# A hybrid decoder block: the gated activations transposed by VectorE in 32x32 squares and by transfers inside SBUF

## The chip, the cores and the metric

The kernel runs on one core of a Trainium2 chip. The metric is device time in microseconds. The core has TensorE (PE, matmul), VectorE (DVE), ScalarE (ACT), GpSimd (POOL) and SyncE (SP, here only an issuer of DMAs); each runs its own instruction stream, and they wait for each other by semaphores.

## The reference

One decoder block over 256 tokens of width 2048, in float32: a gated feed-forward (FFN), a mixer with a convolution group and an attention group, a second FFN, and a final norm. The change is in the two FFNs:

```python
D_MODEL = 2048
SEQ = 256
D_FF = 5632
...
def swiglu(h, wg, wu, wd):
    return (jax.nn.silu(h @ wg) * (h @ wu)) @ wd
...
        x = x + 0.5 * swiglu(rmsnorm(x, ffn1_norm[i]), ffn1_wg[i], ffn1_wu[i], ffn1_wd[i])
        x = x + hybrid_mixer(rmsnorm(x, mix_norm[i]), w_in[i], ...)
        x = x + 0.5 * swiglu(rmsnorm(x, ffn2_norm[i]), ffn2_wg[i], ffn2_wu[i], ffn2_wd[i])
    return rmsnorm(x, final_norm)
```

## The kernel before

**Products in three parts.** Every large product is made of float32r matmuls, with both operands split into a high and a low part: hi x hi, hi x lo and lo x hi (L459, L460, L461). The activations stand transposed in SBUF as the stationary operand (hT_hi, hT_lo for the input of a layer; guT_hi, guT_lo for silu(gate) times up), and the weights stream by as the moving operand.

**Weights in groups.** A group is 256 rows of a weight matrix by 512 columns, 512 KB. Four slots hold groups in three buffers: raw, w_hi, w_lo. SyncE loads a group into raw as soon as VectorE has made w_lo of the group four before it (`load`, L348). ScalarE copies raw to w_hi (`hi`, L841) when the load has landed and TensorE is done with the group four before. VectorE subtracts to get w_lo (`lo`, L1164). TensorE then runs the group's 12 matmuls (`group`, L459 to L461): two row blocks, two token tiles, three products.

**An FFN.** The hidden width is 11 chunks of 512 columns (NFC = 11). For a chunk there is a "gate" job and an "up" job of 8 groups each (JD = 8); gate goes to PSUM banks 0 and 1, up to banks 2 and 3. A hardware loop of 10 passes (`Fori`) holds the up job of chunk i and then the gate job of chunk i + 1; the up job of the last chunk and the "down" jobs (22 groups each, JF = 22, four column blocks) follow behind it. Each engine has the same order of groups written out by hand, with its own side work put in behind a numbered group: `after={1: [...]}` runs something behind group 1 of the job.

**A chunk's side work.** When the gate job is done, ScalarE makes silu of it into gu (`silu`, L887, [128 tokens, 2 tiles, 512]), behind group 1 of the up job. When the up job is done, VectorE multiplies gu by it (`up`, L1213), behind group 1 of the next gate job. Behind group 3 of that gate job TensorE transposes gu with eight 128x128 transposes into banks 4 and 5 (`gu_transposes`, L480 through `transposes`). Behind group 5, ScalarE copies the banks to guT_hi (`gu_operand`, L895) and VectorE subtracts to guT_lo (L1221). For the last chunk the same steps stand in the first down job. The down jobs read guT_hi and guT_lo, and the last chunk's tiles only from group 18 of the first down job on.

```python
                with pe.Fori(0, NFC - 1) as i:
                    job(c, JD, hT_hi, hT_lo, 1, i, 2 * JD)

                    pe.wait_ge(silu_done, count(2 * (NFC * f + 1), i, 2))
                    job(c + JD, JD, hT_hi, hT_lo, 0, i, 2 * JD, after={3: [lambda: gu_transposes(f, 0, i)]})
```

**SyncE's queue** holds nothing but loads in the FFNs: 16 in a loop pass, in the order in which TensorE uses them, each behind its wait for w_lo.

Of the kernel before, what the change touches and what calls it, by code (L numbers as in the profile page):

```python
# [12 lines left out]
P = 128  # L13
TOK = 256
# [15 lines left out]
NCP = 16  # L30
EPS = 1e-6
# [13 lines left out]
Q0, Q1, KS, KW, KC, CC_UP, CH_UP, CB_UP, CH_LO, CB_LO, CC_LO = range(N_IN)  # L45

# [50 lines left out]
def mixer_banks():  # L97
# [20 lines left out]
    first = {4: NDC + NFC + NDC, 5: NDC + NFC + NDC, 6: 0, 7: 0}  # L118
# [12 lines left out]
def build_program(nc, a, out):  # L131
    USE, EXTRA, seen = mixer_banks()

    X_USE = {4: (0, NDC + NFC, seen[4]), 5: (0, NDC + NFC, seen[5])}
    GU_USE = {4: (NDC, seen[4] + NDC), 5: (NDC, seen[5] + NDC)}

    def operand_use(kind, which, b, n=0):

        return {"x": X_USE, "gu": GU_USE}[kind][4 + b][which] + n

# [54 lines left out]
    gu = sb("gu", [P, NT, CH])  # L195

# [64 lines left out]
    with ctx:  # L261
# [28 lines left out]
        gu_done = sem("gu_done")  # L290
        resid_done = sem("resid_done")
# [50 lines left out]
        def _(sp):  # L342
# [17 lines left out]

            def ffn(f):
# [6 lines left out]
                with sp.Fori(0, NFC - 1) as i:  # L368
                    for j in range(JD):
                        load(c + j, wu[f][:, GK * j:GK * j + GK, bass.ds(i * CH, CH)], i, 2 * JD)  # L370
                    for j in range(JD):
                        load(c + JD + j, wg[f][:, GK * j:GK * j + GK, bass.ds(i * CH + CH, CH)], i, 2 * JD)
                c += 2 * JD * (NFC - 1)
# [3 lines left out]
                for n in range(NDC):  # L377
# [3 lines left out]
                    for j in range(JF):  # L381
                        load(c + JF * n + j, wd[f][:, GK * j:GK * j + GK, n * CH:n * CH + CH])

# [60 lines left out]
        def _(pe):  # L444
# [38 lines left out]
            def x_transposes(which, n):  # L483
# [5 lines left out]
                for b in range(2):  # L489
# [4 lines left out]
                    to_bank(4 + b, operand_use("x", which, b, n))  # L494
# [3 lines left out]
            def x_operand(which, j):  # L498

                pe.wait_ge(free[4 + j % 2], operand_use("x", which, j % 2, j // 2) + 1)  # L500

            def gu_transposes(f, n, i=None):
                pe.wait_ge(gu_done, count(2 * (NFC * f + n + 1), i, 2))
                for b in range(2):
                    to_bank(4 + b, operand_use("gu", f, b, n), i, 1)
                    transposes(4 + b, [(kk * TOK + t * P, gu[:, t, (2 * b + kk) * P:][:, 0:P])
                                       for kk in range(2) for t in range(NT)])

            def gu_operand(f, j):
                pe.wait_ge(free[4 + j % 2], operand_use("gu", f, j % 2, j // 2) + 1)  # L510
# [12 lines left out]
            def ffn(f):  # L523
# [11 lines left out]
                with pe.Fori(0, NFC - 1) as i:  # L535
# [3 lines left out]
                    job(c + JD, JD, hT_hi, hT_lo, 0, i, 2 * JD, after={3: [lambda: gu_transposes(f, 0, i)]})  # L539
# [4 lines left out]
                for n in range(NDC):  # L544
                    if n == 0:
                        before = {0: [lambda: gu_operand(f, JF - 4), lambda: gu_operand(f, JF - 3)]}
                        before.update({j: [lambda j=j: gu_operand(f, j)] for j in (JF - 2, JF - 1)})
                        after = {3: [lambda: gu_transposes(f, NFC - 1)]}
                        if f == 0:
                            after[6] = [vector_transposes]  # L550
                    else:
                        before = {}
                        if f == 0:
# [265 lines left out]
        def _(act):  # L819
# [39 lines left out]
            def x_operand(which, n, b=None):  # L859
                vec0 = (V_FFN1, V_MIX, V_FFN2)[which]  # L860
                for b in range(2) if b is None else (b,):
                    scaled_operand(hT_hi, 4 * n + 2 * b, vec0, [(4 + b, operand_use("x", which, b, n))])
# [17 lines left out]
            def silu(f, n, c, i=None):  # L880
# [3 lines left out]
                for b in range(2):  # L884
                    act.wait_ge(full[4 + b], count(operand_use("gu", f, b, n), i, 1))
# [4 lines left out]
            def gu_operand(f, n, i=None):  # L890
                for b in range(2):
                    act.wait_ge(full[4 + b], count(operand_use("gu", f, b, n) + 1, i, 1))
                    k = 4 * n + 2 * b
                    dst = guT_hi[:, k:k + 2, :] if i is None else guT_hi[:, bass.ds(i * 4 + k, 2), :]
                    act.activation(dst, ps[:, 4 + b, :].rearrange("p (k t) -> p k t", k=2),  # L895
                                   ACT.Copy).then_inc(operand_hi, 1)

            def ffn(f):
# [19 lines left out]
                with act.Fori(0, NFC - 1) as i:  # L918
                    job(c, JD, i, 2 * JD, after={1: [lambda: silu(f, 0, c, i)]})
                    job(c + JD, JD, i, 2 * JD, after={5: [lambda: gu_operand(f, 0, i)]})  # L920
# [3 lines left out]
                for n in range(NDC):  # L924
                    if n == 0:
                        after = {5: [lambda: gu_operand(f, NFC - 1)]}
                        if f == 0:
                            after[8] = [vectors]
# [219 lines left out]
        def _(dve):  # L1148
# [25 lines left out]
            OP_X = {0: 0, 1: 2 * (NDC + NFC), 2: 2 * (NDC + NFC + NDC + 2)}  # L1174
            OP_GU = [2 * NDC, OP_X[2] + 2 * NDC]
            OP_ATT = 2 * (NDC + NFC + NDC)
# [39 lines left out]
            def gu_operand(f, n, i=None):  # L1216
                for b in range(2):
                    dve.wait_ge(operand_hi, count(OP_GU[f] + 2 * n + b + 1, i, 2))
                    k = 4 * n + 2 * b
                    sl = slice(k, k + 2) if i is None else bass.ds(i * 4 + k, 2)  # L1220
                    tt(guT_lo[:, sl, :], ps[:, 4 + b, :].rearrange("p (k t) -> p k t", k=2),  # L1221
                       guT_hi[:, sl, :].bitcast(F32), ALU.subtract).then_inc(free[4 + b], 1)
# [19 lines left out]
            def ffn(f):  # L1242
# [13 lines left out]
                with dve.Fori(0, NFC - 1) as i:  # L1256
                    job(c, JD, i, 2 * JD)
                    job(c + JD, JD, i, 2 * JD, after={1: [lambda: up(f, 0, c + JD, i)],
                                                      5: [lambda: gu_operand(f, 0, i)]})
# [3 lines left out]
                for n in range(NDC):  # L1263
                    if n == 0:
                        after = {1: [lambda: up(f, NFC - 1, c)], 5: [lambda: gu_operand(f, NFC - 1)]}
# [424 lines left out]
```

## Time and profile before

| | |
|---|---|
| timed runs | 1924.78 us median of 3 (1923.17 to 1926.34) |
| span of the profiled execution | 1920.8 us |
| PE, PEld busy | 1906.4 us (99%), 1562.8 us (81%) |
| DVE, ACT busy | 997.9 us (52%), 899.3 us (47%) |
| granted TensorE clock, mean | 0.999 |
| DMA | 350.96 MB, mean 183 GB/s |
| transposes of gu on PE (L480) | 176, in 22 blocks of eight |

The profile is one execution, taken by the hardware profiler. PE is the matmuls, PEld the weight loads that overlap them. DVE is VectorE, ACT is ScalarE, SPq is the issue of a DMA by SyncE. A busy PE is not PE at its peak: matmuls overlap, so the distance from one start to the next is what one costs, not its duration. A group of rows reads: line, engine, operation, output and inputs, shapes, count, busy time and mean duration, then the idle time of the engine just before them and who ended it.

### The profile page before, as it was taken

How to read it: one execution, taken by the hardware profiler on the slowest of the kernel's cores; microseconds unless marked ns; L12 is line 12 of the kernel's file. 1: busy time of each engine (PE TensorE's matmuls, PEld its weight loads, DVE VectorE, ACT ScalarE, POOL GpSimd, SP SyncE). 2: the span in 40 equal slices, each digit the busy share in tenths (PEclk: the TensorE clock that was granted, in tenths of full speed). 3: DMA queues.
4: the chain of work that ended last, by engine and by line, in shares of the span. 5: the costliest groups of instructions: out<-in, count | busy, mean ns of one | idle time of the engine just before them, and what ended most of it. 6: DMA issues, size and time to landing. Idle time of an engine off the chain costs nothing.

```text
span 1920.8 us, 23438 instructions
## 1 busy us (share of the span) xinstructions
PE 1906.4 (99%) x8715; PEld 1562.8 (81%) x8715; DVE 997.9 (52%) x1070; ACT 899.3 (47%) x1127; POOL 15.5 (1%) x24
## 2 busy tenths in 40 slices
PE   9999999999999999999999999999999999999998
PEld 7888888888888888887778778888888888888886
DVE  5445544544544444556665776544544445445444
ACT  6444444544444444444454546445444444444443
POOL 1000000000000000000000000000000000000000
PEclk9999999999999999999999999999999999999999
DMA  7555665566555556554435645665565555566664
GB/s 257 192 189 183 188 197 183 179 199 191 190 183 197 196 189 193 172 171 129 114 95 169 187 158 166 199 195 175 187 202 191 192 189 176 196 219 195 192 192 144
DMA packets 185947, 350.96 MB, mean 183 GB/s; under 512 B 13140, under 2 KB 17984, under 8 KB 185760
## 3 DMA queue, kind: packets, MB, share of 16 engines
q1 hardware_dynamic: 183264, 349.22, 56.8%
q8 instruction: 40, 0.66, 0.1%
q10 hardware_dynamic: 2240, 0.47, 0.1%
q0 software_dynamic: 384, 0.47, 0.1%
q14 instruction: 19, 0.16, 0.0%
HBM read 348.01 MB, written 2.10 MB: 182 GB/s over the span
## 4 chain that ended last, share of the span: by engine, by line
PE 97%; DVE 2%; ACT 1%; issue 0%; ACTq 0%; DVEq 0%
PE ps L459 30%; PE ps L461 30%; PE ps L460 30%; PE ps L480 3%; PE ps L625 1%; PE ps L645 1%; DVE w_lo L1164 1%; PE ps L626 0%; ACT w_hi L841 0%; PE ps L519 0%; PE ps L718 0%; DVE p_h L1433 0%; ACT junk L868 0%; DVE x L1229 0%; ACT hT_hi L855 0%
## 5 line engine op out<-in xcount | busy, mean ns | idle before, releaser
L1164 DVE TENSOR_TENSOR w_lo<-raw,w_hi 128x1024 fp32r<-128x1024 f32 x656 | 789.7, 1223 | 662.0 <-ACT w_hi L841 659.7
L841 ACT ACTIVATE w_hi<-raw 128x1024 fp32r<-128x1024 f32 x656 | 682.0, 1060 | 593.3 <-PE ps L461 517.2
L459 PE MATMUL ps<-w_hi,hT_hi 128*128 128x512 f32 x1760 | 690.9, 393 | 1.2 <-DVE w_lo L1164 1.1
L461 PE MATMUL ps<-w_hi,hT_lo 128*128 128x512 f32 x1760 | 685.6, 390 | 0.0
L460 PE MATMUL ps<-w_lo,hT_hi 128*128 128x512 f32 x1760 | 685.3, 389 | 0.0
L459 PEld LDWEIGHTS ps<-w_hi,hT_hi 128*128 128x128 f32 x1760 | 330.8, 188 | 69.1 <-issue 1.4
L461 PEld LDWEIGHTS ps<-w_hi,hT_lo 128*128 128x128 f32 x1760 | 330.4, 188 | 69.1
L460 PEld LDWEIGHTS ps<-w_lo,hT_hi 128*128 128x128 f32 x1760 | 330.7, 188 | 66.5
L459 PE MATMUL ps<-w_hi,guT_hi 128*128 128x512 f32 x704 | 274.5, 390 | 0.0
L461 PE MATMUL ps<-w_hi,guT_lo 128*128 128x512 f32 x704 | 274.0, 389 | 0.0
L460 PE MATMUL ps<-w_lo,guT_hi 128*128 128x512 f32 x704 | 273.9, 389 | 0.0
L461 PEld LDWEIGHTS ps<-w_hi,guT_lo 128*128 128x128 f32 x704 | 132.2, 188 | 27.7
L460 PEld LDWEIGHTS ps<-w_lo,guT_hi 128*128 128x128 f32 x704 | 132.2, 188 | 27.3
L459 PEld LDWEIGHTS ps<-w_hi,guT_hi 128*128 128x128 f32 x704 | 132.2, 188 | 27.1
L1221 DVE TENSOR_TENSOR guT_lo<-ps,guT_hi 128x512 f32 (+1 forms) x44 | 28.4, 686 | 96.9 <-ACT guT_hi L895 96.9
L895 ACT ACTIVATE guT_hi<-ps 128x512 f32 (+1 forms) x44 | 23.9, 594 | 108.1 <-PE ps L480 108.1
L1213 DVE SCALAR_TENSOR_TENSOR gu<-ps,rs,gu 128x512 f32<-128x512 f32 x44 | 31.0, 746 | 70.6 <-PE ps L461 70.6
L887 ACT ACT_TABLE_LOAD x20 | 25.7, 1283 | 86.7 <-PE ps L461 86.7
L1006 ACT ACTIVATE prob<-ps,mins 128x128 f32<-128x128 f32 (+1 forms) x64 | 26.3, 417 | 79.9 <-DVE mins L1378 79.9
L1183 DVE SCALAR_TENSOR_TENSOR hT_lo<-ps,vecs,hT_hi 128x256 fp32r<-128x256 f32 x48 | 20.0, 477 | 36.6 <-ACT hT_hi L855 36.6
L855 ACT ACTIVATE hT_hi<-ps,vecs 128x256 fp32r<-128x256 f32 x48 | 18.9, 475 | 39.1 <-PE ps L480 39.1
L887 ACT ACTIVATE gu<-ps,rs 128x512 f32<-128x512 f32 x44 | 27.8, 685 | 8.9 <-PE ps L461 8.6
(197 smaller groups left out, 799.7 us busy)
## 6 DMA issues: line engine op xcount, KB each, us to landing
raw<-in_ffn_wg_dram SPq DMA_DIRECT2D x176, 512.0 KB, 4.5
raw<-in_ffn_wu_dram SPq DMA_DIRECT2D x176, 512.0 KB, 4.5
raw<-in_ffn_wd_dram SPq DMA_DIRECT2D x176, 512.0 KB, 4.7
raw<-in_w_in_dram SPq DMA_DIRECT2D x88, 512.0 KB, 3.8
raw<-in_w_out_dram SPq DMA_DIRECT2D x32, 512.0 KB, 4.5
raw<-in_cmp_k_w_dram SPq DMA_DIRECT2D x8, 256.0 KB, 3.3
raw<-in_cmp_v_w_dram SPq DMA_DIRECT2D x8, 256.0 KB, 4.0
out_dram<-y_fin SPq DMA_DIRECT2D x8, 256.0 KB, 3.1
```

Of the source, the lines that this page charges most:

```text
L459: mm(o, x_hi, w_hi[:, s, kk, :], start=first and kk == 0, stop=False)
L460: mm(o, x_hi, w_lo[:, s, kk, :], start=False, stop=False)
L461: ins = mm(o, x_lo, w_hi[:, s, kk, :], start=False, stop=last and kk == GK - 1)
L480: ins = pe.transpose(ps[:, bank, o:o + P], src, ident)
L841: act.activation(w_hi[:, c % SLOTS, :, :], raw[:, c % SLOTS, :, :], ACT.Copy).then_inc(hi_ready, 1)
L887: act.activation(gu[:, t, :], ps[:, t, :], ACT.Silu, scale=rs[:, RS_FFN2 if f else RS_FFN1, t:t + 1]).then_inc(silu_done, 1)
L895: act.activation(dst, ps[:, 4 + b, :].rearrange("p (k t) -> p k t", k=2), ACT.Copy).then_inc(operand_hi, 1)
L1006: ins = act.activation(prob[:, m % 2, br * nk:br * nk + nk], ps[:, bank, br * nk:br * nk + nk], ACT.Exp, bias=mins[:, m, br:br + 1], scale ...
L1164: tt(w_lo[:, s, :, :], raw[:, s, :, :], w_hi[:, s, :, :].bitcast(F32), ALU.subtract).then_inc(lo_ready, 1)
L1183: ins = stt(out=lo_t[:, k, :], in0=ps[:, bank, kk * TOK:kk * TOK + TOK], scalar=vecs[:, vec0 + k:vec0 + k + 1], in1=hi_t[:, k, :].bitcast( ...
L1213: stt(out=gu[:, t, :], in0=ps[:, 2 + t, :], scalar=rs[:, RS_FFN2 if f else RS_FFN1, t:t + 1], in1=gu[:, t, :], op0=ALU.mult, op1=ALU.mult) ...
L1221: tt(guT_lo[:, sl, :], ps[:, 4 + b, :].rearrange("p (k t) -> p k t", k=2), guT_hi[:, sl, :].bitcast(F32), ALU.subtract).then_inc(free[4 + ...
```

## The change

gu is no longer transposed by TensorE. VectorE transposes it in squares of 32x32 (`gu_transpose`, behind group 2 of the gate job, two instructions of 128x512, from gu into gu_sq). That leaves each square transposed within its own 32 partitions. SyncE then moves the squares to the partitions where they belong, with 16 DMAs from SBUF to SBUF (`gu_blocks`): for each of the 4 x 4 pairs of partition blocks one DMA of 32 partitions, two tiles and 512 bytes, 32 KB, from gu_sq to gu_raw. They stand in SyncE's queue behind load 6 of the gate job (GU_MOVE), behind a wait for gu_squares. ScalarE copies gu_raw to guT_hi in one instruction, behind group 7 of the gate job (before: from PSUM in two, behind group 5), and VectorE subtracts to guT_lo in one. TensorE waits for gu_done at the end of the gate job, ahead of the next up job, and for gu_lo ahead of the down jobs. For the last chunk the transposes are behind group 2, the moves behind load 6 and the copies behind group 8 of the first down job. The counts of uses of banks 4 and 5 are adapted. The core of the diff (left out: the counts of bank uses, and the names of semaphores):

```diff
@@ -28,6 +28,8 @@
 CMP_BLOCK, CMP_STRIDE, CMP_HID = 32, 16, 256
 NCMP = (TOK - CMP_BLOCK) // CMP_STRIDE + 1
 NCP = 16
+SQ = 32
+QB = P // SQ
 EPS = 1e-6
 BIG = 1e30
...
@@ -43,6 +45,9 @@
 
 IN_COL = [3072, 3584, 4608, 5120, 4096, 2560, 512, 1536, 0, 1024, 2048]
 Q0, Q1, KS, KW, KC, CC_UP, CH_UP, CB_UP, CH_LO, CB_LO, CC_LO = range(N_IN)
+
+
+GU_MOVE = 6
 
 
 def mixer_order():
...
@@ -193,6 +197,8 @@
     guT_hi = sb("guT_hi", [P, KF, TOK], F32R)
     guT_lo = sb("guT_lo", [P, KF, TOK], F32R)
     gu = sb("gu", [P, NT, CH])
+    gu_sq = sb("gu_sq", [P, NT, CH])
+    gu_raw = sb("gu_raw", [P, NT, QB, CH // QB])
 
     at[0] = zone
     y_at = at[0]
...
@@ -358,6 +368,14 @@
                     sp.dma_start(x[:, :, 0:lo], x_in[:, :, 0:lo]).then_inc(x_half_landed, 16)
                 sp.dma_start(x[:, :, lo:n * CH + CH], x_in[:, :, lo:n * CH + CH]).then_inc(x_landed[n], 16)
 
+            def gu_blocks(f, n, i=None):
+
+                sp.wait_ge(gu_squares, count(NFC * f + n + 1, i, 1))
+                for a_ in range(QB):
+                    for c_ in range(QB):
+                        sp.dma_start(gu_raw[c_ * SQ:c_ * SQ + SQ, :, a_, :],
+                                     gu_sq[a_ * SQ:a_ * SQ + SQ, :, c_ * P:c_ * P + P]).then_inc(gu_moved, 16)
+
             def ffn(f):
                 c = FFN0[f]
                 for j in range(JD):
...
@@ -370,6 +388,8 @@
                         load(c + j, wu[f][:, GK * j:GK * j + GK, bass.ds(i * CH, CH)], i, 2 * JD)
                     for j in range(JD):
                         load(c + JD + j, wg[f][:, GK * j:GK * j + GK, bass.ds(i * CH + CH, CH)], i, 2 * JD)
+                        if j == GU_MOVE:
+                            gu_blocks(f, 0, i)
                 c += 2 * JD * (NFC - 1)
                 for j in range(JD):
                     load(c + j, wu[f][:, GK * j:GK * j + GK, (NFC - 1) * CH:FF])
...
@@ -380,6 +400,8 @@
                         sp.dma_start(g_fin[:, :], a["final_norm"].partition_broadcast(P)).then_inc(g_fin_landed, 16)
                     for j in range(JF):
                         load(c + JF * n + j, wd[f][:, GK * j:GK * j + GK, n * CH:n * CH + CH])
+                        if n == 0 and j == GU_MOVE:
+                            gu_blocks(f, NFC - 1)
 
             ffn(0)
             for (job, j), c in AT.items():
...
@@ -491,23 +513,13 @@
                         pe.wait_ge(gains_landed, 16)
                         pe.transpose(ps[:, 6, 0:KD], vec_rows[0:KD, :], consts[0:KD, 0:KD]).then_inc(vecs_full, 1)
                         pe.wait_ge(x_landed[0], 16)
-                    to_bank(4 + b, operand_use("x", which, b, n))
+                    to_bank(4 + b, operand_use(which, b, n))
                     transposes(4 + b, [(kk * TOK + t * P, x[:, t, (4 * n + 2 * b + kk) * P:][:, 0:P])
                                        for kk in range(2) for t in range(NT)])
 
             def x_operand(which, j):
 
-                pe.wait_ge(free[4 + j % 2], operand_use("x", which, j % 2, j // 2) + 1)
-
-            def gu_transposes(f, n, i=None):
-                pe.wait_ge(gu_done, count(2 * (NFC * f + n + 1), i, 2))
-                for b in range(2):
-                    to_bank(4 + b, operand_use("gu", f, b, n), i, 1)
-                    transposes(4 + b, [(kk * TOK + t * P, gu[:, t, (2 * b + kk) * P:][:, 0:P])
-                                       for kk in range(2) for t in range(NT)])
-
-            def gu_operand(f, j):
-                pe.wait_ge(free[4 + j % 2], operand_use("gu", f, j % 2, j // 2) + 1)
+                pe.wait_ge(free[4 + j % 2], operand_use(which, j % 2, j // 2) + 1)
 
             def vector_transposes():
...
@@ -536,20 +548,24 @@
                     job(c, JD, hT_hi, hT_lo, 1, i, 2 * JD)
 
                     pe.wait_ge(silu_done, count(2 * (NFC * f + 1), i, 2))
-                    job(c + JD, JD, hT_hi, hT_lo, 0, i, 2 * JD, after={3: [lambda: gu_transposes(f, 0, i)]})
+                    job(c + JD, JD, hT_hi, hT_lo, 0, i, 2 * JD)
+
+                    pe.wait_ge(gu_done, count(2 * (NFC * f + 1), i, 2))
                 c += 2 * JD * (NFC - 1)
                 job(c, JD, hT_hi, hT_lo, 1)
                 c += JD
                 pe.wait_ge(silu_done, 2 * NFC * (f + 1))
                 for n in range(NDC):
                     if n == 0:
-                        before = {0: [lambda: gu_operand(f, JF - 4), lambda: gu_operand(f, JF - 3)]}
-                        before.update({j: [lambda j=j: gu_operand(f, j)] for j in (JF - 2, JF - 1)})
-                        after = {3: [lambda: gu_transposes(f, NFC - 1)]}
+                        before = {0: [lambda: pe.wait_ge(gu_lo, NFC * f + NFC - 1)],
+                                  JF - 2: [lambda: pe.wait_ge(gu_lo, NFC * f + NFC)]}
+                        after = {}
                         if f == 0:
                             after[6] = [vector_transposes]
                     else:
                         before = {}
+                        if n == 1:
+                            pe.wait_ge(gu_done, 2 * NFC * (f + 1))
                         if f == 0:
                             after = {3: [lambda: x_transposes(1, n - 1)]}
                         else:
...
@@ -881,19 +897,17 @@
 
                 act.wait_ge(group_done, count(c, i, 2 * JD))
                 act.wait_ge(rs_done, (RS_FFN2 if f else RS_FFN1) + 1)
-                for b in range(2):
-                    act.wait_ge(full[4 + b], count(operand_use("gu", f, b, n), i, 1))
                 for t in range(NT):
                     act.activation(gu[:, t, :], ps[:, t, :], ACT.Silu,
                                    scale=rs[:, RS_FFN2 if f else RS_FFN1, t:t + 1]).then_inc(silu_done, 1)
 
             def gu_operand(f, n, i=None):
-                for b in range(2):
-                    act.wait_ge(full[4 + b], count(operand_use("gu", f, b, n) + 1, i, 1))
-                    k = 4 * n + 2 * b
-                    dst = guT_hi[:, k:k + 2, :] if i is None else guT_hi[:, bass.ds(i * 4 + k, 2), :]
-                    act.activation(dst, ps[:, 4 + b, :].rearrange("p (k t) -> p k t", k=2),
-                                   ACT.Copy).then_inc(operand_hi, 1)
+                act.wait_ge(gu_moved, count(16 * QB * QB * (NFC * f + n + 1), i, 16 * QB * QB))
+                k = 4 * n
+                dst = guT_hi[:, k:k + 4, :] if i is None else guT_hi[:, bass.ds(i * 4 + k, 4), :]
+                act.activation(dst.rearrange("p k (g s) -> p k g s", s=SQ),
+                               gu_raw[:, :, :, :].rearrange("p t a (k s) -> p k (t a) s", s=SQ),
+                               ACT.Copy).then_inc(gu_hi, 1)
 
             def ffn(f):
                 c = FFN0[f]
...
@@ -917,15 +931,15 @@
                 c += JD
                 with act.Fori(0, NFC - 1) as i:
                     job(c, JD, i, 2 * JD, after={1: [lambda: silu(f, 0, c, i)]})
-                    job(c + JD, JD, i, 2 * JD, after={5: [lambda: gu_operand(f, 0, i)]})
+                    job(c + JD, JD, i, 2 * JD, after={JD - 1: [lambda: gu_operand(f, 0, i)]})
                 c += 2 * JD * (NFC - 1)
                 job(c, JD, after={1: [lambda: silu(f, NFC - 1, c)]})
                 c += JD
                 for n in range(NDC):
                     if n == 0:
-                        after = {5: [lambda: gu_operand(f, NFC - 1)]}
+                        after = {JD: [lambda: gu_operand(f, NFC - 1)]}
                         if f == 0:
-                            after[8] = [vectors]
+                            after[10] = [vectors]
                     elif f == 0:
                         after = {3: [lambda: x_square(RS_MIX, n - 1, 2 * n)], 5: [lambda: x_operand(1, n - 1)]}
                     else:
...
@@ -1214,12 +1227,19 @@
                         in1=gu[:, t, :], op0=ALU.mult, op1=ALU.mult).then_inc(gu_done, 1)
 
             def gu_operand(f, n, i=None):
-                for b in range(2):
-                    dve.wait_ge(operand_hi, count(OP_GU[f] + 2 * n + b + 1, i, 2))
-                    k = 4 * n + 2 * b
-                    sl = slice(k, k + 2) if i is None else bass.ds(i * 4 + k, 2)
-                    tt(guT_lo[:, sl, :], ps[:, 4 + b, :].rearrange("p (k t) -> p k t", k=2),
-                       guT_hi[:, sl, :].bitcast(F32), ALU.subtract).then_inc(free[4 + b], 1)
+                dve.wait_ge(gu_hi, count(NFC * f + n + 1, i, 1))
+                k = 4 * n
+                sl = slice(k, k + 4) if i is None else bass.ds(i * 4 + k, 4)
+                split = lambda u: u.rearrange("p k (g s) -> p k g s", s=SQ)
+                tt(split(guT_lo[:, sl, :]), gu_raw[:, :, :, :].rearrange("p t a (k s) -> p k (t a) s", s=SQ),
+                   split(guT_hi[:, sl, :].bitcast(F32)), ALU.subtract).then_inc(gu_lo, 1)
+
+            def gu_transpose(f, n, i=None):
+                dve.wait_ge(gu_done, count(2 * (NFC * f + n + 1), i, 2))
+                for t in range(NT):
+                    ins = nc.vector.transpose(gu_sq[:, t, :].rearrange("p (c k s) -> p c k s", c=QB, s=SQ),
+                                              gu[:, t, :].rearrange("p (k c s) -> p c k s", c=QB, s=SQ))
+                ins.then_inc(gu_squares, 1)
 
             def residual(n, done, pair, scale):
...
@@ -1256,13 +1276,15 @@
                 with dve.Fori(0, NFC - 1) as i:
                     job(c, JD, i, 2 * JD)
                     job(c + JD, JD, i, 2 * JD, after={1: [lambda: up(f, 0, c + JD, i)],
-                                                      5: [lambda: gu_operand(f, 0, i)]})
+                                                      2: [lambda: gu_transpose(f, 0, i)],
+                                                      JD - 1: [lambda: gu_operand(f, 0, i)]})
                 c += 2 * JD * (NFC - 1)
                 job(c, JD)
                 c += JD
                 for n in range(NDC):
                     if n == 0:
-                        after = {1: [lambda: up(f, NFC - 1, c)], 5: [lambda: gu_operand(f, NFC - 1)]}
+                        after = {1: [lambda: up(f, NFC - 1, c)], 2: [lambda: gu_transpose(f, NFC - 1)],
+                                 JD: [lambda: gu_operand(f, NFC - 1)]}
                     else:
                         after = {1: [lambda: residual(n - 1, c + JF * n, (n - 1) % 2, half)]}
                         if f == 0:
```

## Rows read from the trace of the kernel before

**Rows 1.** The page: busy times, chain of waits by engine, main DMA queue.

```profile
PE 1906.4 (99%) x8715; PEld 1562.8 (81%) x8715; DVE 997.9 (52%) x1070; ACT 899.3 (47%) x1127; POOL 15.5 (1%) x24
...
q1 hardware_dynamic: 183264, 349.22, 56.8%
...
PE 97%; DVE 2%; ACT 1%; issue 0%; ACTq 0%; DVEq 0%
```

**Rows 2.** The page's costliest groups: busy us, mean ns, idle before.

```profile
L1164 DVE TENSOR_TENSOR w_lo<-raw,w_hi 128x1024 fp32r<-128x1024 f32 x656 | 789.7, 1223 | 662.0 <-ACT w_hi L841 659.7
...
L459 PE MATMUL ps<-w_hi,hT_hi 128*128 128x512 f32 x1760 | 690.9, 393 | 1.2 <-DVE w_lo L1164 1.1
```

**Rows 3.** Timeline of PE around one block: start us, us, instruction.

```profile
244.27 0.40 PE L461 MATMUL ps<-w_hi,hT_lo 128*128 128x512 f32 x1
244.51 1.04 PE L480 MATMUL ps<-consts,gu 128*128 128x128 f32 x8
245.30 0.48 PE L459 MATMUL ps<-w_hi,hT_hi 128*128 128x512 f32 x1
245.62 0.40 PE L460 MATMUL ps<-w_lo,hT_hi 128*128 128x512 f32 x1
```

**Rows 4.** Timeline of ACT over the same loop pass.

```profile
212.18 1.28 ACT L887 ACT_TABLE_LOAD   x1 [4.49 <-PE ps L461]
...
220.88 1.06 ACT L841 ACTIVATE w_hi<-raw 128x1024 fp32r<-128x1024 f32 x1 [2.32 <-DMA raw<-in_ffn_wu_dram]
...
246.22 2.01 ACT L841 ACTIVATE w_hi<-raw 128x1024 fp32r<-128x1024 f32 x2
248.24 1.28 ACT L841 ACT_TABLE_LOAD   x1
249.54 1.06 ACT L841 ACTIVATE w_hi<-raw 128x1024 fp32r<-128x1024 f32 x1
...
256.60 1.28 ACT L887 ACT_TABLE_LOAD   x1 [4.49 <-PE ps L461]
```

**Rows 5.** Timeline of DVE over the same loop pass.

```profile
233.92 1.41 DVE L1213 SCALAR_TENSOR_TENSOR gu<-ps,rs,gu 128x512 f32<-128x512 f32 x2 [3.23 <-PE ps L461]
235.25 3.61 DVE L1164 TENSOR_TENSOR w_lo<-raw,w_hi 128x1024 fp32r<-128x1024 f32 x3
...
250.63 1.23 DVE L1164 TENSOR_TENSOR w_lo<-raw,w_hi 128x1024 fp32r<-128x1024 f32 x1 [0.96 <-ACT w_hi L841]
```

**Rows 6.** SyncE's loads in this pass: two timeline rows, then durations and landing.

```profile
217.10 1.51 SPq L348 DMA_DIRECT2D raw<-in_ffn_wu_dram  x2
...
236.64 1.50 SPq L348 DMA_DIRECT2D raw<-in_ffn_wg_dram  x2
...
L348 SPq DMA_DIRECT2D raw<-in_ffn_wg_dram x8: 372/373/373, 219.4 to 237.8; - x8
...
DMA to landing us min/median/max: 3.6/4.2/5.5
```

**Rows 7.** SyncE's queue: a load at the start, output stores, their landing.

```profile
3.35 0.90 SPq L348 DMA_DIRECT2D raw<-in_ffn_wg_dram  x1
...
1911.10 0.45 SPq L401 DMA_DIRECT2D out_dram<-y_fin  x1
...
1911.59 0.45 SPq L401 DMA_DIRECT2D out_dram<-y_fin  x1
...
DMA to landing us min/median/max: 2.5/3.1/3.5
```

**Rows 8.** Timelines: a w_lo, the weight load it released, one in full flow.

```profile
8.24 1.23 DVE L1164 TENSOR_TENSOR w_lo<-raw,w_hi 128x1024 fp32r<-128x1024 f32 x1
...
9.58 0.19 PEld L459 LDWEIGHTS ps<-w_hi,hT_hi 128*128 128x128 f32 x1 [1.01 <-PE ps L519]
...
244.05 0.19 PEld L461 LDWEIGHTS ps<-w_hi,hT_lo 128*128 128x128 f32 x1
```

**Rows 9.** A VectorE copy of 128x512 inside SBUF.

```profile
L1310 DVE COPY p_h<-p_kvc x2: 420/420/421, 870.5 to 878.6; 128x512 f32<-128x512 f32 x2
```

## The prediction: what TensorE gives up, and what the queues behind it take

> **What bounds the kernel now.** I read the page's busy times and its chain of waits first, then the costliest groups, then one loop pass in order of time on each engine. The reader is to see three things. TensorE is busy for 1906.4 of 1920.8 us, and 97% of the chain that ended last is PE [rows 1]; its largest group waited 1.2 us in all [rows 2]. So only what TensorE executes sets the time. VectorE and ScalarE are about half idle, but they aren't free at every moment: each group of weights needs a 1.06 us w_hi on ScalarE [rows 4] and then a 1.22 us w_lo on VectorE [rows 2] before TensorE may start on it.
>
> One loop pass is 16 groups of 12 matmuls, and in it one block of eight gu transposes. Matmuls start 0.227 us apart, so a group is 2.72 us. The pass itself is 44.42 us from table load to table load on ScalarE (212.18 to 256.60) [rows 4]; 192 x 0.2267 is 43.53, which leaves 0.89 for the block. The timeline agrees: without the block the next L459 would start at 244.50; the L460 behind the block starts at 245.62, so its L459 counts as 245.39: 0.89 [rows 3].
>
> **What is removed.** 22 blocks (11 chunks in each of two FFNs) x 0.89 = 19.6 us of PE, none of it beside other PE work. 1920.8 - 19.6 = 1901.2 for the profiled execution. The median of the timed runs lies 4.0 above that span, and I keep that distance: 1905.2 if nothing new waits.
>
> **What is added, in the order in which it must run.** I count from E, the end of the last group of the "up" job (233.62 in the pass shown: the block starts four groups, 10.88, after it). g0 to g7 are the gate job's groups, g8 the first group of the next pass. Group gk is due at E + 2.72k, and g8 at +21.77.
> - VectorE: both gu products end at +1.71 and w_lo of g2 at +2.85 [rows 5]. Then two transposes of 128x512 in squares of 32x32. The trace has no such instruction. The bounds are a 128x512 copy inside SBUF at 0.42 [rows 9] and a 128x1024 w_lo at 1.22 [rows 2]; nearest are the two 128x512 products, 1.41 for both [rows 5], and as the transpose has one operand less I take 1.3 for two: +4.15. Queued behind them is w_lo of g3, due at +8.16, ready at about +5.4: hidden.
> - SyncE: load g6 is issued when w_lo of g2 is done (236.64, +3.0, 0.37 long) [rows 6]. Then it waits for the transposes and issues 16 moves of 32 KB. The trace has no move inside SBUF. Nearest are the output stores, issued behind each other: 1911.10 and 1911.59, 0.49 apart [rows 7]. Bounds: 0.37, a load that is issued alone [rows 6], and 0.90, the sixth of the transfers queued at the kernel's start, behind 2 MB that hadn't landed [rows 7]. I take 0.49: the stores read SBUF too and nothing large is in front of them. First move +4.25, last one done with at +4.25 + 15 x 0.49 + 0.45 = +12.05.
> - Queued behind the moves on SyncE is load g7. In before it left right behind g6 (both within 1.50 us from 236.64) [rows 6], now at +12.15: 8 us later. ScalarE started on a load 3.78 us after its issue (217.10 to 220.88) [rows 4, 6], so w_hi of g7 starts at +16.0 (before: it was ready when its buffer was). The landing takes 3.6 to 5.5, median 4.2 [rows 6]; I take 3.8 as the moves leave the DMA engines idle by then, and keep 4.5 for the range. w_lo of g7 ends at +18.3 and is due at +18.7: covered by 0.4.
> - The moves have landed before that: the last is issued at +11.6, and a store lands in 2.5 to 3.5 [rows 7]: +15.1 at worst, while ScalarE reaches its wait for them behind w_hi of g7, at +17.
> - ScalarE copies guT_hi in one 128x1024 instruction instead of two halves. By the w_hi form it is 1.06 [rows 4]; two such took 2.01 (246.22), then follow a table load of 1.28 (248.24) at the head of the loop and w_hi of g8 (249.54), whose w_lo ends at 251.86 [rows 4, 5]. That is 5.64 from the start of the first: +16.0 + 5.64 = +21.64 for w_lo of g8. VectorE's own guT_lo of 1.22 fits while the table loads.
> - When must w_lo of g8 be done? The weight load started 0.11 after a w_lo ended (8.24 + 1.23 = 9.47, 9.58) [rows 8], and in a full pipeline a weight load starts 0.22 ahead of its matmul (244.05 and 244.27) [rows 3, 8]. So at +21.77 - 0.33 = +21.44. TensorE waits 0.2 us in each of 20 passes.
>
> **Edits of one answer.** ScalarE's and VectorE's waits for transposes in banks 4 and 5 go, and were idle time off the path (w_hi behind them was the first of three ready at once). The new wait for gu_done at the end of the gate job is met 20 us earlier (+1.71 against +21.77). The last chunk of each FFN has no table load, and its copy stands behind g8: load g7 makes +18.3 against +18.7 there, nothing waits. 11.5 MB of moves (22 x 512 KB) join 349 MB on DMA engines that are busy for 56.8% of the span [rows 1].
>
> **The sum.** 1905.2 + 20 x s, where s is TensorE's wait in a loop pass. With s = 0.2: 1909.2. The whole gain is gone at s = 0.98, and a move spacing x moves s by 15 (x - 0.49) once s is above zero: break-even lies at 0.54 us per issue. The change hangs on that number.
>
> One rule speaks against the change, and one price differs. The rows of the stores show a new issue every 0.49 us while the first ones, which land in 2.5 to 3.5 us, are still on their way [rows 7]: transfers overlap. The Trainium skill, DMA: Bandwidth & Descriptors, section Rules for kernel authors, says to merge many small transfers into one, as under 64 KB they are mostly overhead; by the rows that overhead is issue time here. For the transpose, the Trainium skill, VectorE: DVE Perf Modes, section The three transpose paths, gives 311 ns for a 128x128 of bf16; eight of them, an estimate from that page, are 2.49 us a chunk instead of 1.3, so s = 1.4 and 1933 us.
>
> **The rivals.**
> - Moves cheaper, or the load faster, or all as forecast (s from 0 to 0.45): 1905 to 1914. For it: the rows above, each a median. This is the forecast, 0.42.
> - Part of the gain lost (s 0.45 to 0.78): 1914 to 1921, for instance landing at 4.2 rather than 3.8 (s = 0.6, 1918). For it: 4.2 is the median, and four overdue loads leave at once. 0.19.
> - The wait returns the gain (s 0.78 to 1.17): 1921 to 1929; transposes of 1.0 us each or a landing at 4.5 (s = 0.9 by either, 1923) do it. 0.12.
> - Slower: SyncE's queue becomes the bound. At 0.60 us per issue the 16 moves take 1.65 us longer, s = 1.85, and the time is 1942; it is slower from 0.55 on. Against it: the stores kept 0.49; for it: five to six moves are in flight at a time, more than the stores were, and an issue has taken 0.90 (s = 6.3, 2031, were it all of them; I give that 0.02 within this case) [rows 7]. 0.24, which holds a slow transpose in the same chain too (1.2 us each: s = 1.3, 1931).
> - The moves land one after another, not overlapped: 16 x 2.5 = 40 us [rows 7], ScalarE stands at +44, w_lo of g8 comes some 27 us late in each pass, about 2450 us. The overlapping stores speak against it. 0.01. [...]
> - The change doesn't do what it says: TensorE's time doesn't fall, as the matmuls behind the block would wait for their weights anyway. Against it: VectorE and ScalarE hold ready groups there (three w_lo in a row behind the products, 235.25) [rows 5]. 1925, 0.02.
>
> **How the numbers follow.** About 0.2% (3.9 us) is what a measurement of this kernel can tell from no change. Faster is under 1920.9: 0.42 + 0.19 = 0.61. Same: 0.12 + 0.02 = 0.14. Slower: 0.24 + 0.01 = 0.25. The range goes from 1903 (no wait, and a block worth 0.1 us more) to 1938 (s = 1.65), which leaves about 0.15 above, the 0.90 us issue among it, and 0.02 below. Within it the forecast's own range is 1904 to 1914.
>
> **What the changed profile would show.** No L480 on gu; matmul starts 0.227 us apart over the whole gate job. SyncE: 16 issues behind load g6, to be read for their spacing, and load g7 about 12.1 us behind E. VectorE: two transposes, for their length. ScalarE: a wait for raw of in_ffn_wg ahead of w_hi of g7, at about +16, and no wait for the moves. TensorE: a wait for w_lo at the first group of each loop pass, 0.2 us x 20. The prediction is wrong if the spacing is over 0.54, if landing behind the moves is over 4.6, or if a transpose takes over 1.05.

## The result: 1968.4 us, slower by 2.3%

The changed kernel takes 1968.4 us (median of 4, 1965.1 to 1972.2) beside 1924.0 for the kernel before: ratio 1.0232, 95% interval 1.0217 to 1.0248. The prediction was 1909.2, range 1903 to 1938, chance of slower 0.25. It was wrong in sign and range.

The page of the changed kernel: busy times, the chain that ended last, two groups of matmuls and the issues (columns as in [rows 1, 2]; L481 to L483 are the former L459 to L461, L857 is w_hi, L1178 w_lo, L901 silu, L1226 the gu product, L1240 the 32x32 transposes, L358 the loads, L376 the moves).

```profile
span 1970.4 us, 23312 instructions
...
PE 1905.8 (97%) x8539; PEld 1546.7 (78%) x8539; DVE 1021.1 (52%) x1092; ACT 900.2 (46%) x1105; POOL 15.5 (1%) x24
...
PE 71%; SPq 11%; DMA 6%; DVE 6%; issue 4%; ACT 3%; DVEq 0%; ACTq 0%
...
L481 PE MATMUL ps<-w_hi,hT_hi 128*128 128x512 f32 x1760 | 694.0, 394 | 46.3 <-DVE w_lo L1178 46.3
...
L481 PE MATMUL ps<-w_hi,guT_hi 128*128 128x512 f32 x704 | 276.2, 392 | 4.6 <-DVE w_lo L1178 4.6
...
gu_raw<-gu_sq SPq DMA_DIRECT2D x352, 32.0 KB, 1.9
```

Before, 97% of the chain was PE [rows 1] and the first product's group waited 1.2 us [rows 2]. Now SyncE's queue and the DMAs hold 17% of the chain, and that group waits 46.3 us for w_lo. VectorE makes w_lo, but neither it nor ScalarE is short of time: they are busy for 52% and 46% of the span, before for 52% and 47%. The timelines of one loop pass, SyncE, VectorE and ScalarE, show who is late:

```profile
248.12 10.22 SPq L376 DMA_DIRECT2D gu_raw<-gu_sq  x16
258.62 0.38 SPq L358 DMA_DIRECT2D raw<-in_ffn_wg_dram  x1
259.61 1.61 SPq L358 DMA_DIRECT2D raw<-in_ffn_wu_dram  x3
```

```profile
244.34 1.41 DVE L1226 SCALAR_TENSOR_TENSOR gu<-ps,rs,gu 128x512 f32<-128x512 f32 x2 [3.23 <-PE ps L483]
...
246.80 1.30 DVE L1240 STREAM_TRANSPOSE gu_sq<-gu 128x512 f32<-128x512 f32 x2
...
263.41 1.23 DVE L1178 TENSOR_TENSOR w_lo<-raw,w_hi 128x1024 fp32r<-128x1024 f32 x1 [8.70 <-ACT w_hi L857]
...
266.81 2.36 DVE L1178 TENSOR_TENSOR w_lo<-raw,w_hi 128x1024 fp32r<-128x1024 f32 x2 [1.04 <-ACT w_hi L857]
```

```profile
221.77 1.28 ACT L901 ACT_TABLE_LOAD   x1
...
262.32 1.06 ACT L857 ACTIVATE w_hi<-raw 128x1024 fp32r<-128x1024 f32 x1 [8.87 <-DMA raw<-in_ffn_wg_dram]
263.29 1.04 ACT L908 ACTIVATE guT_hi<-gu_raw 128x1024 f32 x1
264.43 1.28 ACT L857 ACT_TABLE_LOAD   x1
...
267.75 1.28 ACT L901 ACT_TABLE_LOAD   x1
```

The 16 moves hold SyncE for 10.22 us. Only then does load g7 leave (258.62). ScalarE idles 8.87 us until it has landed, and TensorE waits twice in the pass, at g7 and at g8 (timeline of PE):

```profile
264.69 0.50 PE L481 MATMUL ps<-w_hi,hT_hi 128*128 128x512 f32 x1 [1.46 <-DVE w_lo L1178]
...
268.09 0.50 PE L481 MATMUL ps<-w_hi,hT_hi 128*128 128x512 f32 x1 [0.37 <-DVE w_lo L1178]
```

### The profile page after: what moved, and what is told of

It reads as the page before. It is cut to its first block, busy times and chain, and to the rows that moved or that the text cites. A ratio compares the mean times of both kernels' runs of the same rounds, so it can differ in the third digit from the quotient of the medians.

```text
span 1970.4 us, 23312 instructions
## 1 busy us (share of the span) xinstructions
PE 1905.8 (97%) x8539; PEld 1546.7 (78%) x8539; DVE 1021.1 (52%) x1092; ACT 900.2 (46%) x1105; POOL 15.5 (1%) x24
## 4 chain that ended last, share of the span: by engine, by line
PE 71%; SPq 11%; DMA 6%; DVE 6%; issue 4%; ACT 3%; DVEq 0%; ACTq 0%
PE ps L481 22%; PE ps L483 22%; PE ps L482 22%; SPq L376 11%; DMA raw<-in_ffn_wu_dram 4%; DVE w_lo L1178 2%; PE ps L502 2%; ACT w_hi L857 1%; DVE gu_sq L1240 1%; PE ps L641 1%; DMA raw<-in_ffn_wg_dram 1%; DVE gu L1226 1%; PE ps L661 1%; ACT L857 1%; SPq L358 0%
## 5 line engine op out<-in xcount | busy, mean ns | idle before, releaser
L1178 DVE TENSOR_TENSOR w_lo<-raw,w_hi 128x1024 fp32r<-128x1024 f32 x656 | 791.5, 1222 | 784.9 <-ACT w_hi L857 783.8
L857 ACT ACTIVATE w_hi<-raw 128x1024 fp32r<-128x1024 f32 x656 | 683.8, 1059 | 833.2 <-PE ps L483 597.6
L481 PE MATMUL ps<-w_hi,hT_hi 128*128 128x512 f32 x1760 | 694.0, 394 | 46.3 <-DVE w_lo L1178 46.3
L483 PE MATMUL ps<-w_hi,hT_lo 128*128 128x512 f32 x1760 | 686.2, 390 | 0.0
L481 PEld LDWEIGHTS ps<-w_hi,hT_hi 128*128 128x128 f32 x1760 | 331.1, 188 | 129.7 <-DVE w_lo L1178 60.1
L483 PEld LDWEIGHTS ps<-w_hi,hT_lo 128*128 128x128 f32 x1760 | 330.7, 188 | 69.7
L481 PE MATMUL ps<-w_hi,guT_hi 128*128 128x512 f32 x704 | 276.2, 392 | 4.6 <-DVE w_lo L1178 4.6
L483 PE MATMUL ps<-w_hi,guT_lo 128*128 128x512 f32 x704 | 275.6, 392 | 0.0
L481 PEld LDWEIGHTS ps<-w_hi,guT_hi 128*128 128x128 f32 x704 | 133.2, 189 | 33.1 <-DVE w_lo L1178 5.3
L483 PEld LDWEIGHTS ps<-w_hi,guT_lo 128*128 128x128 f32 x704 | 133.2, 189 | 28.0
L1226 DVE SCALAR_TENSOR_TENSOR gu<-ps,rs,gu 128x512 f32<-128x512 f32 x44 | 31.0, 747 | 70.6 <-PE ps L483 70.6
L901 ACT ACTIVATE gu<-ps,rs 128x512 f32<-128x512 f32 x44 | 27.9, 685 | 6.1 <-PE ps L483 5.9
L481 PE MATMUL ps<-w_hi,ycT_hi 128*128 128x512 f32 x64 | 26.7, 417 | 3.4 <-DVE w_lo L1178 3.4
L641 PE MATMUL ps<-kT,qT 64*128 64x256 f32 (+1 forms) x64 | 29.1, 534 | 0.0
```

Of the source, the lines that this page charges most:

```text
L481: mm(o, x_hi, w_hi[:, s, kk, :], start=first and kk == 0, stop=False)
L483: ins = mm(o, x_lo, w_hi[:, s, kk, :], start=False, stop=last and kk == GK - 1)
L641: mm(o, qT[rows_, jp * GRP + r, t * P:t * P + P], kT[rows_, jp, :, 0:nk], start=True, stop=False)
L857: act.activation(w_hi[:, c % SLOTS, :, :], raw[:, c % SLOTS, :, :], ACT.Copy).then_inc(hi_ready, 1)
L901: act.activation(gu[:, t, :], ps[:, t, :], ACT.Silu, scale=rs[:, RS_FFN2 if f else RS_FFN1, t:t + 1]).then_inc(silu_done, 1)
L1178: tt(w_lo[:, s, :, :], raw[:, s, :, :], w_hi[:, s, :, :].bitcast(F32), ALU.subtract).then_inc(lo_ready, 1)
```

## The experiments

Each kernel is the changed one with the edit shown, beside runs of the kernel before on the same chip (1923.5 for e1 to e4, 1923.8 for e5, e6 and the two v kernels). The ratios are to that kernel before; the changed kernel's 1968.4 stands beside 1924.0.

**The moves left out, and the moves merged.** My theory after the result: the 16 issues hold SyncE's queue, and all else costs nothing.

```diff
-                act.wait_ge(gu_moved, count(16 * QB * QB * (NFC * f + n + 1), i, 16 * QB * QB))
+                act.wait_ge(gu_squares, count(NFC * f + n + 1, i, 1))
...
-                        if j == GU_MOVE:
-                            gu_blocks(f, 0, i)
```

> The changed kernel without its 352 moves: ScalarE and VectorE read gu_sq, the untransposed blocks, so the down jobs work on misplaced numbers. Theory (the moves hold SyncE's queue, and through it the loads): with them gone TensorE has lost its 22 blocks at 0.89 us and waits for nothing new, 1905 us (1903 to 1908). Rival (the two transposes on VectorE or the 128x1024 copies behind group 7 are late by themselves): 1915 or more, with waits for w_lo at groups 7 and 8.

Measured: 1904.4 us, ratio 0.9897 (0.9881 to 0.9914). The pass takes 43.52 us where before took 44.42: 0.90 less, and TensorE waits for w_lo in a handful of places, as before:

```profile
PE ps L477 <- DVE w_lo L1174: 5.1, 5, 1.5
PEld ps L477 <- DVE w_lo L1174: 2.2, 2, 1.9
```

The whole gain of the removed block is there, with both transposes and the 128x1024 copies in place. The rival, that the transposes or the larger copies are late by themselves, is out.

```diff
-                    for c_ in range(QB):
-                        sp.dma_start(gu_raw[c_ * SQ:c_ * SQ + SQ, :, a_, :],
-                                     gu_sq[a_ * SQ:a_ * SQ + SQ, :, c_ * P:c_ * P + P]).then_inc(gu_moved, 16)
+                    for h_ in range(2):
+                        sp.dma_start(gu_raw[a_ * SQ:a_ * SQ + SQ, :, 2 * h_:2 * h_ + 2, :].rearrange("p t a m -> p t (a m)"),
+                                     gu_sq[(a_ + 1) % QB * SQ:(a_ + 1) % QB * SQ + SQ, :,
+                                           h_ * 2 * P:h_ * 2 * P + 2 * P]).then_inc(gu_moved, 16)
```

> The same 512 KB per chunk in 8 moves of 64 KB instead of 16 of 32 KB (32 partitions, two tiles, 1 KB each; blocks land in wrong places, so the down jobs work on misplaced numbers). Theory (a fixed issue time per DMA, 0.60 us and 0.64 from start to start): 8 fewer issues give 5.1 us back, more than the 2.5 that a pass lacks: 1905 us (1903 to 1910), issue still 0.60. Rival (the issue takes as long as its bytes or descriptors): 1.2 us each, 1965 us.

Measured: 1903.7 us, ratio 0.9899 (0.9882 to 0.9915). The moves of this kernel (count: duration ns min/median/max):

```profile
L376 SPq DMA_DIRECT2D gu_raw<-gu_sq x176: 585/596/744, 60.5 to 1662.3; - x176
```

Twice the bytes each, and the issue still takes 0.60. So the count costs, not the bytes: the same 512 KB a chunk in half as many DMAs brings the whole gain.

**A smaller dose.**

```diff
-                    for c_ in range(QB):
+                    for c_, w_ in ((0, 1), (1, 1), (2, 1), (3, 1)) if a_ < 2 else ((0, 1), (1, 1), (2, 2)):
```

> 14 moves instead of 16 for the same 512 KB (two of them 64 KB; blocks in wrong places, so the down jobs work on misplaced numbers). Theory (each issue is 0.64 us of SyncE's queue, and TensorE waits for what is over): load g7 leaves 1.3 us earlier than in the changed kernel, at +13.3; w_lo of g7 is then 0.6 late and that of g8 1.25: s = 1.5 a pass, 1934 us (1922 to 1946). Rival (a threshold or a cost that isn't in proportion, as a full queue): 1905 or 1968.

Measured: 1934.4 us, ratio 1.0061 (1.0045 to 1.0078), on the 1934 expected. 0, 8, 14 and 16 issues a chunk give 1904.4, 1903.7, 1934.4 and 1968.4: nothing for the first eight, and from 14 to 16 it is 17 us for each issue more. Where between 8 and 14 the rise begins was not measured. 20 passes and two last chunks x 0.64 would be 14.1; the rest is what the later sections find, the second wait and the clock.

**Where the issue time comes from.** The forecast took 0.49 from stores to HBM. If that row was the wrong one to take, because a move has both its ends in SBUF, then the same 16 DMAs out of HBM must give about the forecast's own time.

```diff
-                                     gu_sq[a_ * SQ:a_ * SQ + SQ, :, c_ * P:c_ * P + P]).then_inc(gu_moved, 16)
+                                     x_in[a_ * SQ:a_ * SQ + SQ, :, c_ * P:c_ * P + P]).then_inc(gu_moved, 16)
```

> The changed kernel with the 16 moves of each chunk read from the input x in HBM instead of gu_sq in SBUF: same count, shape, bytes, place in the queue and waits; the down jobs work on wrong numbers. Theory (what the forecast had wrong is the issue time of a DMA with both ends in SBUF, 0.60 and 0.64 from start to start; out of HBM it is 0.43 and 0.47): the sum of the prediction holds with x = 0.47, load g7 leaves at about +11.8, s is 0 to 0.2: 1904 to 1909 us. Rival (16 small DMAs cost this whatever they read: number of instructions, transfers in flight, semaphore writes): 1955 to 1968 us.

Measured: 1906.6 us, ratio 0.9913 (0.9896 to 0.9929). One row on the moves, and TensorE's waits:

```profile
L376 SPq DMA_DIRECT2D gu_raw<-in_x_dram x352: 316/427/577, 59.6 to 1667.4; - x176
...
PEld ps L481 <- DVE w_lo L1178: 6.2, 9, 1.9
PE ps L481 <- DVE w_lo L1178: 5.6, 8, 1.5
```

Same count, shape, bytes and waits, 62 us faster. The DMAs land 1.9 us after their issue in both kernels (median), so out of HBM, issued closer together, no fewer are in flight. The cost is not the number of instructions alone and not the transfers in flight, but the 0.17 us more that each issue takes when both ends are SBUF. The probe series, issued one behind another at the end of the program, say what it hangs on:

> The changed kernel with six series of eight DMAs on SyncE's queue behind the output stores: the move's own form; one row of 256 per partition in SBUF; the same shape of 32 partitions out of HBM; 128 partitions inside SBUF; 128 partitions out of HBM; 32 partitions of 1 KB rows. Time: 1968 plus the series, some 50 us. If the issue time hangs on both ends being SBUF, the first, second, fourth and sixth series take 0.60 and those out of HBM 0.45 to 0.47. If it hangs on the number of partitions, the third takes 0.60 and the fourth 0.47. If on the two tiles as a second dimension, the second alone is shorter.

```profile
L434 SPq DMA_DIRECT2D x<-gu_sq x8: 591/596/597, 1968.6 to 1973.0; - x8
...
L434 SPq DMA_DIRECT2D x<-gu_sq x8: 565/590/592, 1974.9 to 1979.3; - x8
...
L434 SPq DMA_DIRECT2D x<-in_x_dram x8: 348/427/428, 1981.2 to 1984.4; - x8
...
L434 SPq DMA_DIRECT2D x<-gu_sq x8: 604/622/704, 1986.4 to 1991.4; - x8
...
L434 SPq DMA_DIRECT2D x<-in_x_dram x8: 399/470/904, 1993.6 to 1997.1; - x8
...
L434 SPq DMA_DIRECT2D x<-gu_raw x8: 596/597/659, 2004.1 to 2008.7; - x8
```

In this order: the move's form 0.60; one row of 1 KB per partition 0.59; the move's form out of HBM 0.43; 128 partitions inside SBUF 0.62; 128 partitions out of HBM 0.47; 32 partitions of 1 KB rows 0.60. Both ends in SBUF is what costs. 128 partitions instead of 32 add 0.03 inside SBUF and up to 0.04 out of HBM (where the rows were also twice as long); the second dimension adds nothing that shows. The kernel ran once, in 2012.9 us.

**Moves behind load 7.** The cheapest mend, one number.

```diff
-GU_MOVE = 6
+GU_MOVE = 7
```

> The moves stand behind load 7 of the gate job instead of load 6. Theory of the queue: load g7 leaves at +5.3 as in the kernel before, the moves end at about +16.0 and the first load of the next pass leaves at +16.2, its w_hi starts at +19.9 and its w_lo ends at +22.2 against +21.4: s = 0.8 us a pass, 1921 us (1914 to 1928), and one wait a pass for w_lo instead of two. Rival (the moves themselves, their bytes or ScalarE's wait for their landing, set the delay wherever they stand): 1960 or more.

Measured: 1981.3 us, ratio 1.0297 (1.0280 to 1.0315). My number was wrong by 60 us, and the time alone fits the rival, 1960 or more. The rows tell the two apart. They are of one pass, where E is 248.11: SyncE, ScalarE, VectorE and PE.

```profile
253.92 10.22 SPq L376 DMA_DIRECT2D gu_raw<-gu_sq  x16
264.77 13.58 SPq L358 DMA_DIRECT2D raw<-in_ffn_wu_dram  x8
```

```profile
265.55 1.06 ACT L908 ACTIVATE guT_hi<-gu_raw 128x1024 f32 x1 [5.31 <-DMA gu_raw<-gu_sq]
268.60 1.28 ACT L857 ACT_TABLE_LOAD   x1 [1.99 <-DMA raw<-in_ffn_wu_dram]
269.90 2.00 ACT L857 ACTIVATE w_hi<-raw 128x1024 fp32r<-128x1024 f32 x2
...
270.99 2.36 DVE L1178 TENSOR_TENSOR w_lo<-raw,w_hi 128x1024 fp32r<-128x1024 f32 x2 [2.99 <-ACT w_hi L857]
...
272.26 0.50 PE L481 MATMUL ps<-w_hi,hT_hi 128*128 128x512 f32 x1 [2.24 <-DVE w_lo L1178]
```

Load g8 left at +16.7 (expected +16.2), and there is one wait instead of two, as the theory of the queue has it. ScalarE does wait 5.31 us for the moves, but that isn't what holds it up: its copy is done at 266.61, and it then idles 1.99 us more for load g8. Two things were left out of the expectation. The table load at the head of the loop stands behind the wait for this very load, so it doesn't run while the load is under way: landing, 1.28, 1.06 and 1.23 come one after another, and g8 starts 2.4 late. And TensorE's wait of 2.24 is followed by a fall of its granted clock (same kernel, windows of 1 us: PE busy and matmuls started stand first, the last three columns are granted clock, DMA share, GB/s):

```profile
272.00:273.00 1.00, 0.73 (x3) 0.65 (x4) 1.00 (x2) 1.00 (x1) 0.00 (x0) 1.00 0.12 45
273.00:274.00 1.00, 1.00 (x4) 0.81 (x4) 0.35 (x1) 0.99 (x3) 0.00 (x0) 0.68 0.51 72
274.00:275.00 1.00, 1.00 (x4) 0.71 (x4) 0.00 (x0) 1.00 (x2) 0.00 (x0) 0.50 0.82 287
...
276.00:277.00 1.00, 1.00 (x5) 0.76 (x4) 1.00 (x2) 0.47 (x2) 0.00 (x0) 0.62 0.78 289
277.00:278.00 1.00, 1.00 (x6) 0.83 (x5) 0.82 (x2) 0.96 (x1) 0.00 (x0) 1.00 0.17 35
```

The clock is at half (1.2 instead of 2.4 GHz) for some 3 us, and the matmuls' starts are 0.43 apart instead of 0.227. From its first matmul to that of the next, a pass takes 47.5 to 48.0 us in 15 of the 20. Two passes of the second FFN have such a wait too (2.27 and 2.08 us) but hold no fall of the clock, and take 45.95 and 45.93. So the late load costs 2.4 us over 43.52 and the clock 1.6 to 2.1 on top: the expected 0.8 became 4.0 to 4.5. The moves cost more in this place because of what the late load met there.

**Eight moves elsewhere.** All 16 moves are made, eight of them from ScalarE's program, behind group 4 of the gate job.

```diff
+                act.wait_ge(gu_squares, count(NFC * f + n + 1, i, 1))
+                for a_ in range(QB // 2, QB):
+                    for c_ in range(QB):
+                        act.dma_start(gu_raw[c_ * SQ:c_ * SQ + SQ, :, a_, :],
+                                      gu_sq[a_ * SQ:a_ * SQ + SQ, :, c_ * P:c_ * P + P]).then_inc(gu_moved, 16)
```

> All 16 moves, eight from SyncE's queue behind load 6 and eight from ScalarE's queue behind w_hi of group 4 of the gate job. Theory: SyncE is free at +9.2, as with eight moves; ScalarE is held from +4.1 to about +9.3, and its w_hi of g5, due in w_lo at +13.3, ends at +10.4: nothing waits, 1904 us (1902 to 1908). Rival (both queues take their descriptors from one generator, so that issues from both at a time take twice as long): both are held to about +14.3, w_lo of g5 is 3 us late: 1965 or more.

Measured: 1903.0 us (1902.7 to 1905.2), ratio 0.9893 (0.9876 to 0.9909).

```profile
234.85 5.43 SPq L376 DMA_DIRECT2D gu_raw<-gu_sq  x8
...
234.85 5.13 ACTq L917 DMA_DIRECT2D gu_raw<-gu_sq  x8
...
PE ps L481 <- DVE w_lo L1187: 5.5, 5, 1.5
```

Both queues issue at the same time, and the rival's doubling is not there. Eight moves from SyncE alone take 5.11 us (e3_eight_moves); here one of the two queues takes as long and the other 0.3 more, SyncE in the first FFN (5.43) and ScalarE in the second. The twin has GpSimd's queue in place of ScalarE's (with a semaphore of its own, and constants in place of the loop):

> All 16 moves, eight from SyncE's queue behind load 6 and eight from GpSimd's queue, which has nothing else to do in the FFNs. Theory: with GpSimd's issues at 0.5 to 0.75 us they are out by +10.5 and land by +13, while ScalarE needs them at +17: nothing waits, 1904 us (1902 to 1908). Rival (GpSimd's transfers land late, or take over 1.4 us each): a wait for the moves on ScalarE at group 7 and 1910 to 1960 us.

Measured: 1904.4 us, ratio 0.9902 (0.9886 to 0.9919). GpSimd's issues take 0.54, ScalarE waited once for a move:

```profile
L459 POOL DMA_DIRECT2D gu_raw<-gu_sq x176: 539/539/549, 60.6 to 1662.1; - x176
...
ACT guT_hi L924 <- DMA gu_raw<-gu_sq: 2.3, 1, 2.3
```

Both are faster than the kernel before and the changed one, by 1.0 to 1.1% and 3.3%; between the two there is no difference that these runs can tell.

## Why the prediction was wrong, point by point

- **What bounds the kernel, and what is removed**: right. 0.89 a block was forecast, the pass without moves is 0.90 shorter than before, and 19.0 us of the 19.6 show (1923.5 to 1904.4).
- **Transposes**: 1.30 for two, as taken. The Trainium skill, VectorE: DVE Perf Modes, section The three transpose paths, has 311 ns for a 128x128 of bf16. Eight of those, an estimate from that page of the Trainium skill, would have been 2.49. Here two instructions of 128x512 float32 do the work in 1.30, and the measurement decides.
- **First move**: +4.07 for +4.25 (E is 244.05, 0.29 ahead of the products, as before).
- **The issue of a move: the step that failed.** "I take 0.49: the stores read SBUF too and nothing large is in front of them." It is 0.60 long and 0.64 from start to start. A store has one end in SBUF, a move has two, and no row of before has such a DMA. The text put the break-even at 0.54 and said that the change hangs on that number, and the measured spacing lies beyond it. The bounds, 0.37 and 0.90, held it, but 0.49 was taken with far too much weight. e5_from_hbm shows that with the HBM form's issue time the sum comes out (1904 to 1909 for 1906.6), e3_eight_moves and e6_fourteen that the count does it.
- **Load g7**: +14.57 for +12.15, 2.42 later. 15 x 0.15 makes 2.25 of that, the last issue's own length 0.15 and a longer step to the load 0.2, less the 0.18 by which the first move came early. Its landing took 3.70 for 3.78, the moves landed in 1.9 for at most 3.5, the copy took 1.04 for 1.06. From the start of w_hi of g7 to the end of w_lo of g8 it is 5.7 for 5.64.
- **The wait per pass**: the formula, 0.2 + 15 (x - 0.49), gives 2.45 at x = 0.64. The pass shown has 45.98 - 43.52 = 2.46. That it fits so well is luck, for the pass is among the shortest. From the first matmul of a pass to that of the next the 20 passes take 45.5 to 48.3, 46.4 on average, 2.9 over 43.52. TensorE's second wait is 0.30 to 1.26, mostly over 0.6, where the pass shown has 0.37. In most passes load g8 lands behind g7 so late that the table load waits for it, as in the next pass (ScalarE, then PE):

```profile
310.90 1.28 ACT L857 ACT_TABLE_LOAD   x1 [0.69 <-DMA raw<-in_ffn_wu_dram]
...
314.56 0.50 PE L481 MATMUL ps<-w_hi,hT_hi 128*128 128x512 f32 x1 [0.98 <-DVE w_lo L1178]
```

  The forecast counted load g7 only. The 20 passes together are 57.4 us over e1_no_moves where the formula has 49.0; the 8.4 more are this second lateness and, in the first pass, the clock. With the formula alone the kernel would take 1954 us; it took 1965.1 to 1972.2.
- **The last chunks, forecast to wait for nothing**: TensorE waits 1.80 us in the first FFN's and 2.76 us in the second's (the 4.6 of the guT_hi group on the page). Group 7 had 0.4 of cover there, and load g7 was more than 2 late. In the second FFN's a single move took 1.41 us, and the 16 took 11.31 instead of 10.2.
- **A cost that wasn't in the sum**: the clock. It fell to half behind the wait of 2.93 us in the first pass and behind both waits in the last chunks. Outside the loop passes the profiled run is 10.1 us longer than that of e1_no_moves: 4.6 of it are those two waits, and most of the rest is the clock behind them. The last fall, in windows of 4 us (PE, PEld, DVE, ACT, POOL busy, granted clock, DMA share, GB/s):

```profile
1732.00:1736.00 4.00, 4.00 (x19) 3.14 (x17) 0.00 (x0) 0.00 (x0) 0.00 (x0) 1.00 0.57 153
1736.00:1740.00 4.00, 1.24 (x4) 0.86 (x4) 2.24 (x2) 3.16 (x4) 0.00 (x0) 0.77 1.02 389
1740.00:1744.00 4.00, 4.00 (x11) 3.13 (x10) 3.62 (x4) 1.80 (x2) 0.00 (x0) 0.50 0.82 250
1744.00:1748.00 4.00, 4.00 (x17) 3.24 (x16) 1.23 (x1) 1.46 (x2) 0.00 (x0) 0.87 0.79 270
```

  11 matmuls started in the third window and 19 in the first. Mean granted clock: 0.995, before 0.999. The profiled run is the slowest of the four; the others had 0.997 to 0.999.
- **The rival "slower: SyncE's queue becomes the bound"** named the mechanism and priced 0.60 per issue at 1942. It had 0.24. Its argument against itself, that the stores kept 0.49, was the same wrong row. Its argument for, that many in flight would slow the issue, is not what happened: e5_from_hbm has at least as many in flight.
- **The rule against the change**, the Trainium skill, DMA: Bandwidth & Descriptors, Rules for kernel authors (coalesce many small transfers; under 64 KB they are mostly overhead), was set aside as "overhead is issue time here". That reading was right and its weight wrong: merged to 64 KB the moves cost nothing (e3_eight_moves, 1903.7 us). The trace agrees with the rule.

What stays open: why the issue takes 0.17 us more with both ends in SBUF, why one move took 1.41 us, and what decides whether the clock falls behind a wait of some 2 us.

## What to carry to other kernels

A queue that feeds the bound engine has a slack in microseconds; count the instructions added to it, not their bytes, and price each by a row with the same two ends (SBUF to SBUF isn't SBUF to HBM). When the sum changes sign within the spread of one price, that price is the forecast: give its upper end the weight, or spread the issues over queues that have nothing due. And follow the second thing that is late as far as the first: here the next load, the table load behind its wait, and the clock.

## What the runs showed of the hardware

- Issue time on SyncE for DMAs behind each other: SBUF to SBUF 0.59 to 0.62, HBM to SBUF 0.43 (32 partitions) and 0.47 (128), SBUF to HBM 0.45 [rows 7], with 0.04 between them; 32 or 64 KB makes no difference. On ScalarE's queue a move took 0.62 (median), on GpSimd's 0.54. With SyncE and ScalarE issuing side by side, eight moves took 5.1 us on one queue and 5.4 on the other, against 5.11 alone on SyncE.
- A 32 KB move inside SBUF lands 1.9 us after its issue (median), and one of 64 KB 2.0.
- VectorE transposes 128x512 float32 in squares of 32x32 in 0.69 us, two of them back to back in 1.30.
- Behind waits of TensorE of 1.80, 2.76 and 2.93 us in the changed kernel, and behind 16 of 2.07 to 2.65 in e2_behind_7, the granted clock fell to 0.50 for 3 to 7 us. In the FFNs of these two kernels it stayed at 1.00 behind all waits of 1.70 and less, but also behind two of 2.10 and 2.27 in e2_behind_7, so the length of the wait alone doesn't decide it.
